# First mixture of experts: the rows of the last expert added by a matrix product, the gather of the others issued before that expert, and the even output projection done by token halves

## The chip, the core and the metric

The kernel runs on one core of a Trainium2 chip, in 32-bit floats. The metric is the device time of one execution in microseconds (us). Engines are named as in the profile: PE multiplies matrices (PEld is its weight load), DVE and ACT are the vector and scalar engines, POOL issues the indirect transfers, SP issues most of the weight loads.

## What is computed

Two networks run on 256 tokens each, one behind the other. The second has two blocks, and in its first block 256 latent and 256 context tokens go through an "even" mixer, whose output projection is added to the token stream, and then through a mixture of 16 experts, of which each token takes two. The change lies in that first block.

```python
def moe(h, router_w, router_b, w1, w3, w2):
    scores = jax.nn.sigmoid((h @ router_w).astype(jnp.float32))
    ...                                        # two experts of the best group of four, and their shares
    y = jnp.zeros_like(h)
    for e in range(N_EXPERTS):
        y = y + comb[:, e:e + 1] * ((jax.nn.silu(h @ w1[e]) * (h @ w3[e])) @ w2[e])
    return y

# second_block, l = 0
        x_lat = x_lat + g1 * o_lat             # o = [attention heads, mLSTM heads] @ w_out
        h_lat = modulate(x_lat, norm_ffn_g[l], sh2, sc2).reshape(B * S, D)
        ...
            x_ctx = x_ctx + cg1 * o_ctx
            h_ctx = modulate(x_ctx, norm_ffn_g[l], csh2, csc2).reshape(B * L, D)
            y = moe(jnp.concatenate([h_lat, h_ctx], axis=0), router_w, router_b, exp_w1[l], exp_w3[l], exp_w2[l])
            y_lat = y[:B * S]
            x_ctx = x_ctx + cg2 * y[B * S:].reshape(B, L, D)
        x_lat = x_lat + g2 * y_lat.reshape(B, S, D)
```

`modulate` is a root-mean-square norm over the 1024 features, times a gain, plus a shift.

## The kernel before

Each engine runs an instruction list written out by hand in program order; semaphores connect them. An engine never passes an instruction that waits. The token stream is `x_t`, features on partitions in eight blocks of 128, 512 tokens along the row: columns 0 to 255 are the context half, 256 to 511 the latent half. PSUM is used as four families of two banks, `proj`, `score`, `turn` and `outp`. `claim(f)` on PE takes the next bank of a family once the bank's earlier use is drained, and `take(f)` on a reader waits until it is filled. Weights of 1 MB come through a ring of six slots that SP fills in order. SP may load a slot again when its last reader is done.

**Even output projection** (`slot_out`, `out_projection`). Each of four ring slots holds 256 output columns, so PE runs two banks of 512 tokens for each, 16 matmuls (32 recorded instructions, since a matmul of 32-bit floats is recorded as two). DVE adds each bank, gated, to `x_t` (`add_gated`, L2770). ACT squares the new `x_t`; PE sums the squares over features with ones (L732, L739); ACT takes the root; DVE takes the reciprocal and multiplies, in two halves of 256 tokens (`normalise`, L2339 and L2583); ACT applies gain and shift (`shift`, L1944). Only then comes the router's product (L1490), then ACT's copy of the logits (L1760), four small matmuls and the sigmoid (L1760 again), and on DVE a chain of some forty small steps that picks two experts for each token, gives it a row in each expert's list (`row_of`, up to 96 rows for an expert) and counts.

**First mixture** (`experts(0)`). POOL scatters the tokens' rows to `xrow_d` in HBM (`expert_in`), and loads them again expert by expert. SP waits until the first such load has landed before it loads expert 1's weights. For each expert PE does `gate` (into `proj`), `hidden` of the up weights (into `score`), `act_turned` (transposes the product) and `output` (into `outp`, rows of 96 tokens packed in four strips of 32 partitions, L1348). Expert e's output stands behind the up product of expert e+1. SP loads gate, up and then the previous expert's output weights (L3281), each when the same place in the ring was last used. The last two loads are expert 15's output weights, issued when its gate product is done. ACT copies each expert's rows (`rows_out`) and stores them to `yrow_d` (`expert_out`).

**After the last expert** POOL waits for all stores, then issues eight indirect gathers (two for each block of 128 tokens, in the order 2, 3, 0, 1, latent first) into `h_tok` and `y_two`. ACT scales one (L2220), DVE adds the other (`mix`, L3037), PE transposes (`mixed_turned`, L1663), DVE adds to `x_t` (`add_mixed`, L3047). The latent half is normed first; then the next block's input projection starts: six steps c = 0 to 5 of one PE product each. At c = 0 the context half's norm follows the product. From c = 1 on, `turn_pairs(c - 1)` follows it: sums of squares for head c - 1 and a rotation product (L664, into `outp`), from which DVE (L3074, L3076, L3077, a reciprocal L2589, L3086) makes the finished head and signals `head_ready`. SP loads these products' weights (`in_odd_w_in`, L3263) once all four blocks are mixed.

If an expert is chosen by more than 96 tokens, a branch (`overflow`) handles the rest. Each engine reads the count and branches (L1311 on PE).

## Time and profile before

| | us |
|---|---|
| median of the 3 runs | 1568.49 |
| lowest, highest | 1566.29, 1568.64 |
| the profiled execution | 1571.42 |
| its span in the trace | 1569.7 |
| PE busy | 1460.4 (93%) |
| DVE, ACT, POOL busy | 560.5, 346.3, 99.5 |

Busy time of an engine says how much it does, not whether anybody waits for it. The chain that ended last names, step by step, what released the next instruction; the timeline gives starts and lengths. Times of day below are microseconds from the span's start. The granted clock stands in the rows as a share of full speed: 1.00 is 2.4 GHz, 0.50 is 1.2 GHz.

The stretches that matter here: the even output projection runs from about 714 to 780, norm and routing to about 816, the 16 experts to about 1112, the gather and mixing to about 1143, and the projection steps c = 0 to 5 to about 1203.

### The profile page before, as it was taken

The page shows a single profiled execution, that of the slowest core. Times are in us where ns is not written, and L with a number is a line of the kernel's source. Part 1 is how long each engine was busy: PE and PEld are TensorE (multiplying, and loading weights), DVE is VectorE, ACT ScalarE, POOL GpSimd, SP SyncE. Part 2 cuts the span into 40 slices and gives each one's busy share as a digit, 9 for nine tenths or more (in the row PEclk, how much of TensorE's full clock was granted, in tenths as well). Part 3 has the DMA queues.
Part 4 walks back from the last instruction along what each step waited for, and adds up shares of the span by engine and source line. Part 5 has one row for each costly group of instructions (what it writes and reads, how often), then busy time and mean ns, then how long its engine had stood idle before and what let it go on. Part 6 is the DMA issues. An engine that isn't in the chain of part 4 may idle for free.

```text
span 1569.7 us, 27108 instructions
## 1 busy us (share of the span) xinstructions
PE 1460.4 (93%) x11433; PEld 1036.6 (66%) x11433; DVE 560.5 (36%) x1380; ACT 346.3 (22%) x804; POOL 99.5 (6%) x152
## 2 busy tenths in 40 slices
PE   7999999999999999999967999999599989899997
PEld 5687677876744767564346999989365666555554
DVE  2615412355155157253150111111266823233233
ACT  2313302133231132262040000100242313000010
POOL 0010100100300000220010000000200001000000
PEclk9999999999999999999979999999799999999999
DMA  8463763735964610655218999999591055999997
GB/s 283 115 215 108 228 195 100 230 120 192 297 205 149 202 54 28 215 182 197 81 64 322 363 399 400 391 398 408 195 364 64 1 187 199 383 382 393 376 384 282
DMA packets 189275, 367.05 MB, mean 234 GB/s; under 512 B 20140, under 2 KB 146952, under 8 KB 173312
## 3 DMA queue, kind: packets, MB, share of 16 engines
q1 hardware_dynamic: 172736, 323.30, 58.3%
q0 software_dynamic: 10544, 32.48, 6.5%
q10 hardware_dynamic: 5904, 9.98, 1.7%
q8 instruction: 66, 1.08, 0.3%
q14 instruction: 25, 0.20, 0.0%
HBM read 345.33 MB, written 20.41 MB: 233 GB/s over the span
## 4 chain that ended last, share of the span: by engine, by line
PE 78%; DMA 10%; DVE 6%; ACT 3%; issue 2%; POOL 1%; SPq 0%; POOLq 0%; ACTq 0%; DVEq 0%
PE ps_proj L664 29%; PE ps_proj L1348 8%; PE ps_outp L664 7%; PE ps_outp L1348 7%; PE ps_score L1348 6%; DMA ring<-in_exp_w 6%; PE ps_outp L1293 4%; PE ps_outp L1449 2%; PE ps_score L848 1%; PE ps_turn L827 1%; PE ps_proj L800 1%; PE ps_proj L912 1%; PE ps_proj L1198 1%; DMA expert_in<-arena,row_of 1%; PE ps_score L908 1%
## 5 line engine op out<-in xcount | busy, mean ns | idle before, releaser
L664 PE MATMUL ps_proj<-h_t,ring 128*128 128x256 f32 (+1 forms) x1184 | 323.8, 431 | 6.5 <-DVE h_t L2437 3.9
L664 PEld LDWEIGHTS ps_proj<-h_t,ring 128*128 128x128 f32 x1184 | 224.8, 192 | 97.6 <-issue 68.4
L1348 PE MATMUL ps_proj<-ring,arena 128*32 128x384 f32 (+2 forms) x1760 | 118.8, 387 | 7.9 <-DMA ring<-in_exp_w 4.9
L1348 PEld LDWEIGHTS ps_proj<-ring,arena 128*32 128x32 f32 (+1 forms) x1760 | 103.9, 115 | 23.6 <-issue 9.9
L1348 PE MATMUL ps_score<-ring,arena 128*32 128x384 f32 (+2 forms) x1760 | 115.1, 381 | 4.1 <-DMA ring<-in_exp_w 4.1
L1348 PE MATMUL ps_outp<-ring,arena 128*32 128x384 f32 (+2 forms) x1504 | 112.7, 417 | 3.5 <-DVE arena L2794 2.1
L1348 PEld LDWEIGHTS ps_score<-ring,arena 128*32 128x32 f32 (+1 forms) x1760 | 98.2, 113 | 20.4 <-issue 8.7
L664 PE MATMUL ps_proj<-ring,h_t 128*128 128x256 f32 x448 | 100.4, 381 | 0.4 <-ACT arena L1969 0.4
L1348 PEld LDWEIGHTS ps_outp<-ring,arena 128*32 128x32 f32 (+1 forms) x1504 | 81.8, 114 | 27.1 <-DVE arena L2794 3.8
L664 PEld LDWEIGHTS ps_proj<-ring,h_t 128*128 128x128 f32 x448 | 84.1, 190 | 15.6 <-issue 4.8
L1760 ACT ACTIVATE arena<-ps_proj 128x512 f32<-128x512 f32 (+1 forms) x68 | 38.5, 569 | 248.9 <-PE ps_proj L664 241.6
L2819 DVE TENSOR_TENSOR arena<-ps_outp,arena 128x512 f32<-128x512 f32 x62 | 40.0, 687 | 94.4 <-PE ps_outp L1449 94.4
L2996 DVE COPY arena<-ps_score 128x384 f32<-128x384 f32 x16 | 8.9, 558 | 152.4 <-PE ps_score L1603 152.4
L2589 DVE RECIPROCAL rstd<-root 128x512 f32<-128x512 f32 x14 | 46.9, 3353 | 43.2 <-ACT root L1760 43.0
L1293 PE MATMUL ps_outp<-arena,ring 128*128 128x512 f32 x128 | 57.8, 609 | 3.0 <-DVE x_t L2770 2.1
L3118 POOL DMA_DIRECT2D modulation_parts<-ada_out x48 | 27.1, 567 | 514.4 <-ACT ada_out L1823 514.4
L664 PE MATMUL ps_outp<-h_t,ring 128*128 128x256 f32 x256 | 56.7, 381 | 2.2 <-DMA ring<-in_w_out 1.4
L664 PEld LDWEIGHTS ps_outp<-h_t,ring 128*128 128x128 f32 x256 | 48.2, 190 | 10.2 <-issue 3.9
L2193 ACT ACTIVATE arena<-ps_outp 128x384 f32<-128x384 f32 x32 | 15.7, 490 | 171.7 <-PE ps_outp L1348 171.7
L1293 PEld LDWEIGHTS ps_outp<-arena,ring 128*128 128x128 f32 x128 | 24.6, 195 | 35.3 <-issue 34.3
L1766 ACT ACTIVATE h_t<-x_t 128x512 f32<-128x512 f32 (+1 forms) x28 | 18.3, 685 | 125.9 <-DVE x_t L2770 60.9
L1811 ACT ACTIVATE both_probs<-ps_score,negmax 128x128 f32<-128x128 f32 (+1 forms) x64 | 30.7, 483 | 65.6 <-DVE negmax L2409 39.4
(403 smaller groups left out, 1848.9 us busy)
## 6 DMA issues: line engine op xcount, KB each, us to landing
ring<-in_exp_w SPq DMA_DIRECT2D x138, 1024.0 KB, 11.4
ring<-in_ada_w SPq DMA_DIRECT2D x48, 1024.0 KB, 5.5
ring<-in_w_in SPq DMA_DIRECT2D x30, 1024.0 KB, 6.5
arena<-in_exp_w SPq DMA_DIRECT2D x24, 1024.0 KB, 15.4
ring<-in_even_w_in SPq DMA_DIRECT2D x12, 1024.0 KB, 6.5
ring<-in_w_out SPq DMA_DIRECT2D x8, 1024.0 KB, 10.1
row_store<-in_exp_w SPq DMA_DIRECT2D x8, 1024.0 KB, 15.6
x_t<-in_exp_w SPq DMA_DIRECT2D x16, 512.0 KB, 15.7
```

Of the source, the lines that this page charges most:

```text
L664: last = pe.matmul(out, w, a, start=(i == 0), stop=(i == len(pairs) - 1))
L800: last = pe.matmul(b[q:q + 32, half * 256:(half + 1) * 256], cond[:, k, :], w[:, k, :], start=(k < 4), stop=(k >= 4))
L1293: last = pe.matmul(b[c][:, :], w[:, k, c * P:(c + 1) * P], nq_t[:, k, :] if k < 4 else ym_t[:, k - 4, :], start=(k == 0), stop=(k == 7))
L1348: last = pe.matmul(b[p0:p0 + pn, c0:c0 + wn], x_of(p0, lo, pn), w(w0, wn), start=first and p0 not in strip[:i], stop=done and p0 not in st ...
L1449: pe.matmul(b[:, :], pick_t[at:at + 64, t * P:(t + 1) * P], y_rows[at:at + 64, 0:512], start=True, stop=True).then_inc(filled[f], 1)
L1760: act.activation(out, src, func, **kw).then_inc(drained["proj"], 1)
L1766: act.activation(h[:, 2 * q:2 * q + 2, :], x_t[:, 2 * q:2 * q + 2, t0:t0 + n], ACT.Square).then_inc(sq_ready, 1)
L1811: ins = act.activation(dst[:, lo:hi], b[:, lo:hi], ACT.Exp, scale=sign, bias=negmax[:, u % 2, q:q + 1], accum_out=total[:, u % 2, q:q + 1])
L2193: act.activation(y_rows[:, q * wide:(q + 1) * wide], bank["outp"][(o0 + q) % 2][:, 0:wide], ACT.Copy).then_inc(drained["outp"], 1)
L2589: step(dve.reciprocal(rstd[:, :], root[:, i % 2, :]))
L2819: dve.tensor_tensor(o, b[:, :], o, ALU.add).then_inc(drained[f], 1)
L3118: pool.dma_start(ada_d[k // 12, s, :, i * 512:(i + 1) * 512], ada_out[s:P:32, k % 2, :]).then_inc(ada_stored[k % 2], 16)
```

## The change

It has four parts.

1. In the even output projection slot 0 is as before. For slots 1 to 3 all context halves come first, then all latent halves, 256 tokens in one bank each. Sums, norm, shift and the transposes of the context half are put between and behind the latent products; behind the end only the latent half is left. The sigmoid's small matmuls go ahead of the remaining transposes.
2. Expert 15's output goes into 96 partitions times two banks of 512 columns (`last_output`: three strips instead of four), is copied to `y_rows` and stays there. DVE builds, ahead of the expert loop, a slot-by-token matrix of the shares of expert 15 (`last_apart`), PE transposes it (`last_pick_turned`), and PE adds `y_rows` times that matrix in PSUM (`last_rows`), together with the other rows, which are turned by a matmul with the identity (`other_rows`). Tokens of expert 15 get share 0 in the gather and a row of another expert.
3. POOL gathers when the 15 other experts are stored. To have these rows early, PE does expert 14's output ahead of expert 15's up product. SP waits for the latent gathers only, and for the mixing before the later weights.
4. The mixing works on halves of 256 tokens. The context half is mixed behind the product of c = 0, and its norm stands behind c = 1 instead of c = 0. ACT takes up that norm at c = 2, once head 0 is finished.

```diff
+            def half_sums(s):
+
+                b = claim("proj")
+                for q in range(4):
...
+            for i in range(1, 4):
+                w = out_weights(i)
+                b = claim("outp")
+                out_part(b, w, HALF[0], 0)
+                out_part(b, w, HALF[0], 1).then_inc(filled["outp"], 1)
+            for i in range(1, 4):
+                w = slot_view((out_slot + i) % RING, KC, 256)
+                b = claim("outp")
+                out_part(b, w, HALF[1], 0)
+                if i == 2:
+                    sum_quarters(S)
+                out_part(b, w, HALF[1], 1).then_inc(filled["outp"], 1)
+                done_with("outp")
+                if i == 1:
+                    half_sums(0)
+            mark["x_even"] = use["outp"]
+            pe.wait_ge(ctx_shifted, KC)
+            tokens_turned(0)
+            half_sums(1)
+            squared[0] += 8
+            sum_quarters(S, S)
+            tokens_turned(1)
...
+                        for q in range(2):
+                            if half == 0:
+                                pe.wait_ge(drained["outp"], o0 + q - 1 + 2 * e)
+                            parts = [(p, 32, p, 0, 512 * q, 512) for p in (0, 32, 64)]
+                            for k in (2 * half, 2 * half + 1):
+                                last = strips(bank["outp"][(o0 + q) % 2], parts, act_of(k),
...
                 gate(e)
                 act_turned(e - 1)
+                output(e - 1)
+                use["turn"] += 2 * EXPERTS
+                last_pick_turned()
                 hidden(e, "score", 2)
-                output(e - 1)
                 act_turned(e)
-                output(e, True)
+                last_output(e)
...
+            def last_rows(s, p):
+
+                f, lo = MIX_BANKS[p], S * (1 - s)
+                b = claim(f)
+                for j in range(2):
+                    c = (2 * p + j) * P
+                    pe.matmul(b[:, j * S:(j + 1) * S], y_rows[0:CAP[0], c:c + P], last_pick_t[0:CAP[0], lo:lo + S],
+                              start=(j == 0), stop=False)
+                mark["mix", s, p] = use[f]
...
+            def other_rows(s, banks):
+
+                for i in range(2):
+                    pe.wait_ge(mixed, 2 * s + i + 1)
+                    for p in range(4):
+                        for j in range(2):
+                            c = (2 * p + j) * P
+                            last = pe.matmul(banks[p][:, j * S + i * P:j * S + (i + 1) * P],
+                                             h_tok[:, TOKEN_BLOCKS[2 * s + i], c:c + P], ident, start=False,
...
             experts(0)
-            for i in range(3):
-                mixed_turned(i)
-            norm(h2[:, :, S:T2], S)(0, 4)
-            mixed_turned(3)
+            banks = [last_rows(0, p) for p in range(4)]
+            other_rows(0, banks)
+            lat_norm = norm(h2[:, :, S:T2], S)
+            banks = []
+            for p in range(4):
+                banks.append(last_rows(1, p))
+                lat_norm(p, p + 1)
...
                 if c == 0:
-                    norm(h2[:, :, 0:S], S)(0, 4)
+                    other_rows(1, banks)
                 if c >= 1:
                     turn_pairs(c - 1)
+                if c == 1:
+                    norm(h2[:, :, 0:S], S)(0, 4)
...
+                    half_square(2, 0, 1)
+                    half_square(2, 0, 0)
+                    for q in range(1, 4):
+                        half_square(2 + q, q, 1)
+                    evac(root[:, 1, 0:S], n=S)
+                    half_square(6, 1, 0)
+                    evac(root[:, 0, 0:S], ACT.Sqrt, S, scale=1.0 / D, bias=EPS)
+                    half_square(7, 2, 0)
+                    for c in range(KC):
+                        xn[0] += 1
+                        act.wait_ge(xn_ready, xn[0])
+                        act.activation(h[:, c, 0:S], h[:, c, 0:S], ACT.Identity, scale=gain[:, 0, 1, 1, c:c + 1],
+                                       bias=mod[:, 0, 3 * KC + c, 1:2]).then_inc(ctx_shifted, 1)
+                    tokens_out(0, 0)
+                    half_square(8, 3, 0)
+                    tokens_out(0, 4)
+                    evac(root[:, 1, S:T2], n=S)
+                    evac(root[:, 0, S:T2], ACT.Sqrt, S, scale=1.0 / D, bias=EPS)
+                    for c in (0, 4):
+                        tokens_out(1, c)
+                    shift(h, 0, 1, S, 1)
+                    warm_up(ACT.Sigmoid)
+                    b = take("score")
+                    act.activation(logit_t[:, 0:n], b[:, 0:n], ACT.Copy).then_inc(drained["score"], 1)
...
-                rows_out(EXPERTS - 1)
+                e = EXPERTS - 1
+                act.wait_ge(y_stored, 32 * e)
+                for q in range(2):
+                    act.wait_ge(filled["outp"], o0 + q + 1 + 2 * e)
+                    act.activation(y_rows[0:cap, q * 512:(q + 1) * 512], bank["outp"][(o0 + q) % 2][0:cap, :], ACT.Copy
+                                   ).then_inc(drained["outp"], 1)
...
+            def stream_weighted(s):
+
+                for t in TOKEN_BLOCKS[2 * s:2 * s + 2]:
+                    act.wait_ge(gathered[t], 32)
+                    act.activation(h_tok[:, t, :], h_tok[:, t, :], ACT.Identity, scale=part[:, 0, t:t + 1]
...
+            stream_weighted(0)
+            stream_squares(0)
             rms_root(S)
             stream_shift(0)
-            stream_squares(1, mark["moe_done", 0])
+            stream_weighted(1)
             for c in range(6):
                 if c == 1:
+                    stream_squares(1)
+                if c == 2:
+                    act.wait_ge(head_ready, 9)
                     rms_root(S)
...
+            for i in range(1, 4):
+                add_half(i, 1)
+            add_half(1, 0)
+            normalise_half(1)
+            add_half(2, 0)
+            add_half(3, 0)
...
+                def last_apart():
...
+                    step(dve.scalar_tensor_tensor(out=row_f, in0=away, scalar=-float((EXPERTS - 1) * CAP[0]), in1=row_f,
+                                                  op0=ALU.mult, op1=ALU.add))
+                    dve.tensor_copy(row_back[:, :, :], row_f).then_inc(back_ready, 1)
+                    step(dve.tensor_tensor(away_part, away, part, ALU.mult))
+                    dve.tensor_tensor(part, part, away_part, ALU.subtract).then_inc(part_ready, 1)
...
+                    for t in range(nb):
+                        ins = dve.tensor_scalar(last_pick[:, t, :], cst("slot")[:, 0:cap], last_place[:, t:t + 1],
+                                                last_share[:, t:t + 1], ALU.is_equal, ALU.mult)
...
                 rows_in(2)
+                last_apart()
...
+                use["turn"] += 2 * EXPERTS
+                b = take("turn")
+                dve.tensor_copy(last_pick_t[0:cap, :], b[0:cap, :]).then_inc(drained["turn"], 1)
...
             experts(0)
             mix(0)
             mix(1)
             add_mixed(0)
+            normalise(h2[:, :, S:T2], S)
             mix(2)
+            mix(3)
             add_mixed(1)
...
             for c in range(6):
+                if c == 1:
+                    for cols in rms(S):
+                        for k in range(KC):
+                            dve.tensor_tensor(h2[:, k, 0:S], x_t[:, k, 0:S], rstd[:, cols], ALU.mult).then_inc(xn_ready, 1)
...
-                pool.wait_ge(y_stored, 32 * EXPERTS)
+                pool.wait_ge(back_ready, 1)
...
-                    gather(yrow_d[0:EXPERTS * CAP[l], :])
+                    pool.wait_ge(y_stored, 32 * (EXPERTS - 1))
+                    gather(yrow_d[0:(EXPERTS - 1) * CAP[l], :])
...
             for entry, n in zip(stream, first_slot):
                 if entry == "early":
+                    sp.wait_ge(filled["outp"], mark["moe_done", 0])
                     for i in range(EARLY):
                         block_load(n, i)
                     continue
...
                 if l == 0:
-                    sp.wait_ge(mixed, T2 // P)
+                    sp.wait_ge(gathered[TOKEN_BLOCKS[1]], 32)
```

The order of instructions shows three places. The first is PE behind the output projection's third slot. `h_t` holds the squares, L674 of the changed program is the plain product (before, L1293), L742 and L749 are the sums (before, L732 and L739). Before:

```order
L1293 MATMUL ps_outp<-arena,ring 128x512 [waits outp_drained,ring_loaded1,proj_drained]
L1293 MATMUL ps_outp<-arena,ring 128x512 x15
L732 MATMUL ps_proj<-h_t,const 32x512 [waits sq_ready]
L732 MATMUL ps_proj<-h_t,const 32x512
L1293 MATMUL ps_outp<-arena,ring 128x512 [waits outp_drained,ring_loaded2]
L1293 MATMUL ps_outp<-arena,ring 128x512 x15
```

Changed, from the last latent product on:

```order
L674 MATMUL ps_outp<-arena,ring 128x256 [waits outp_drained]
L674 MATMUL ps_outp<-arena,ring 128x256 x7
L749 MATMUL ps_proj<-root,const 128x256 [waits proj_drained]
L674 MATMUL ps_outp<-arena,ring 128x256 x8
L674 MATMUL ps_outp<-arena,ring 128x256 [waits outp_drained]
L674 MATMUL ps_outp<-arena,ring 128x256 x15
L1323 MATMUL ps_proj<-const,h_t 128x128 [waits proj_drained,ctx_shifted]
```

The context half's sum now stands inside the products, and its transposes directly behind them.

The second place is PE at expert 15. `ring_loaded5` and `ring_loaded0` are the up weights of expert 15, `ring_loaded1` and `ring_loaded2` the output weights of expert 14; rows that continue a product are left out. Before:

```order
L1603 MATMUL ps_score<-const,arena 128x128 x2
L1348 MATMUL ps_score<-ring,arena 32x384 [waits ring_loaded5]
L1348 MATMUL ps_score<-ring,arena 32x384 x2
...
L1348 MATMUL ps_score<-ring,arena 32x384 [waits ring_loaded0]
...
L1348 MATMUL ps_outp<-ring,arena 32x384 [waits outp_drained,ring_loaded1,score_drained]
L1348 MATMUL ps_outp<-ring,arena 32x384 x2
```

Changed:

```order
L1667 MATMUL ps_score<-const,arena 128x128 x2
L1404 MATMUL ps_outp<-ring,arena 32x384 [waits outp_drained,ring_loaded1,score_drained]
...
L1404 MATMUL ps_outp<-ring,arena 32x384 [waits ring_loaded2]
...
L1691 MATMUL ps_turn<-const,arena 96x128 [waits turn_drained,last_pick_ready]
L1691 MATMUL ps_turn<-const,arena 96x128 x3
L1404 MATMUL ps_score<-ring,arena 32x384 [waits ring_loaded5]
```

The product that needs the weights loaded later now stands ahead of the one whose weights are loaded first.

The third place is ACT and PE at steps c = 1 and 2 of the projection. ACT, changed: `root<-ps_proj 128x512` finishes head 0's root; the two rows behind it are the context norm, `head_ready` is DVE's signal that head 0 is done.

```order
L2060 ACTIVATE arena<-ps_proj 128x512 [waits proj_filled]
L2421 ACTIVATE arena<-ps_proj,vec 128x512
L1867 ACTIVATE root<-ps_proj 128x512 [waits proj_filled,head_ready]
L1867 ACTIVATE root<-ps_proj 128x256 [waits proj_filled,head_ready]
L1867 ACTIVATE root<-ps_proj 128x256 [waits proj_filled]
L2392 ACTIVATE h_t<-h_t,mod,gain 128x256 [waits xn_ready] x8
```

PE, changed, from `turn_pairs(0)` on; `proj_drained` of L749 is the first of these two ACT rows:

```order
L674 MATMUL ps_proj<-arena,const 128x512 [waits proj_drained,head_sq_ready]
L674 MATMUL ps_outp<-arena,const 128x512 [waits outp_drained,proj_drained]
L742 MATMUL ps_proj<-h_t,const 32x256 [waits sq_ready,proj_drained]
...
L749 MATMUL ps_proj<-root,const 128x256 [waits proj_drained]
L674 MATMUL ps_proj<-h_t,ring 128x256 [waits proj_drained,ring_loaded5]
L674 MATMUL ps_proj<-h_t,ring 128x256 x15
```

Before, the ACT rows of the same norm stood ahead of head 0's root, with no wait for `head_ready`:

```order
L1953 ACTIVATE arena<-ps_proj 128x512 [waits proj_filled]
L2253 ACTIVATE arena<-ps_proj,vec 128x512
L1760 ACTIVATE root<-ps_proj 128x256 [waits proj_filled] x2
L2237 ACTIVATE h_t<-h_t,mod,gain 128x256 [waits xn_ready] x8
L1953 ACTIVATE arena<-ps_proj 128x512 [waits proj_filled]
```

The context norm moved behind head 0, and PE's product of c = 2 stands behind that norm's second sum.

## Rows read from the trace of the kernel before

**Rows 1.** The chain that ended last: start, us, engine, result, line, instructions
```profile
831.87 3.69 DMA arena<-expert_in
...
1121.62 6.14 DMA arena<-expert_out,row_of
...
1143.61 7.52 PE ps_proj L664 x32
...
1278.24 7.12 PE ps_outp L664 x32
```

**Rows 2.** Timeline, output projection: start, us, instruction, count, idle before
```profile
751.51 13.97 PE L1293 MATMUL ps_outp<-arena,ring 128*128 128x512 f32 x32 [1.06 <-DVE x_t L2770]
...
780.56 0.88 DVE L2770 SCALAR_TENSOR_TENSOR x_t<-ps_outp,mod,x_t 128x256 f32<-128x256 f32 x2 [2.56 <-PE ps_outp L1293]
```

**Rows 3.** Timeline, end of the second half's shift, and the sigmoid
```profile
793.59 4.04 ACT L1944 ACTIVATE h_t<-h_t,mod,gain 128x256 f32<-128x256 f32 x8 [0.43 <-DVE h_t L2583]
...
801.41 0.22 ACT L1760 ACTIVATE arena<-ps_proj 128x64 f32<-128x64 f32 x1 [0.43 <-PE ps_proj L1503]
```

**Rows 4.** SP's two loads of expert 14's output weights (line L3281, 1089.7 to 1091)
```profile
L3281 SPq DMA_DIRECT2D ring<-in_exp_w x2: 383/384/384, 1089.5 to 1090.1; - x2
...
DMA to landing us min/median/max: 9.7/10.7/11.8
```

**Rows 5.** Timeline of PE: expert 15 up, expert 14 output, expert 15 output
```profile
1094.98 5.45 PE L1348 MATMUL ps_score<-ring,arena 128*32 128x384 f32 x96
...
1100.16 5.46 PE L1348 MATMUL ps_outp<-ring,arena 128*32 128x384 f32 x80
...
1106.75 5.41 PE L1348 MATMUL ps_outp<-ring,arena 128*32 128x384 f32 x80 [0.65 <-DVE arena L2996]
```

**Rows 6.** Timeline, then windows: length, busy by engine, clock, DMA, GB/s
```profile
859.62 7.10 PE L1348 MATMUL ps_proj<-ring,arena 128*32 128x384 f32 x96 [3.80 <-DMA ring<-in_exp_w]
...
859.00:860.00 1.00, 0.38 (x5) 0.34 (x9) 0.00 (x0) 0.00 (x0) 0.00 (x0) 0.82 0.95 393
...
1113.00:1143.00 30.00, 9.80 (x50) 6.47 (x50) 13.51 (x31) 9.06 (x13) 7.93 (x8) 0.60 0.62 209
```

**Rows 7.** Timeline of PE, expert 0: up product, then its output with nothing between
```profile
826.03 5.50 PE L1348 MATMUL ps_score<-ring,arena 128*32 128x384 f32 x96
...
833.45 5.41 PE L1348 MATMUL ps_outp<-ring,arena 128*32 128x384 f32 x80 [0.65 <-DVE arena L2996]
```

**Rows 8.** PE's branch on the count: lengths in ns, starts
```profile
L1311 PEldq COMPARE_BRANCH  x2: 340/398/456, 1113.8 to 1567.2; - x2
```

**Rows 9.** Timeline, gathers, mixing and the latent norm
```profile
1117.78 1.01 POOL L3249 DMA_INDIRECT arena<-expert_out,row_of  x1 [50.38 <-issue]
...
1124.48 1.15 ACT L2220 ACTIVATE arena<-arena 128x1024 f32<-128x1024 f32 x1 [11.78 <-DMA arena<-expert_out,row_of]
...
1125.74 1.28 DVE L3037 SCALAR_TENSOR_TENSOR arena<-arena 128x1024 f32<-128x1024 f32 x1 [19.04 <-ACT arena L2220]
...
1134.24 1.28 ACT L1793 ACT_TABLE_LOAD   x1
...
1135.64 2.17 ACT L1766 ACTIVATE h_t<-x_t 128x512 f32<-128x512 f32 x4
...
1138.98 0.38 ACT L1760 ACTIVATE root<-ps_proj 128x256 f32<-128x256 f32 x1 [1.17 <-PE ps_proj L732]
...
1142.86 4.05 ACT L2237 ACTIVATE h_t<-h_t,mod,gain 128x256 f32<-128x256 f32 x8 [2.28 <-DVE h_t L2583]
```

**Rows 10.** Timeline, norm sums; c = 2 and head 0's rotation
```profile
1151.05 1.07 PE L732 MATMUL ps_proj<-h_t,const 128*32 128x256 f32 x16
...
1161.81 7.07 PE L664 MATMUL ps_proj<-h_t,ring 128*128 128x256 f32 x32
1162.08 0.69 DVE L3074 TENSOR_TENSOR arena<-ps_outp,const 128x512 f32<-128x512 f32 x1 [3.72 <-PE ps_outp L664]
...
1167.65 0.69 DVE L3086 TENSOR_TENSOR arena<-arena,rstd 128x512 f32<-128x512 f32 x1
```

249 lines of the change are left out of this document (162 added, 87 removed).

## Prediction

> **What bounds the kernel now.** I read the chain that ended last first. It says who releases whom in the stretches that the change touches: PE's output projection, then ACT and DVE through norm and routing, then the scattered rows coming back from HBM (a load of 3.69 us that ends at 835.56), PE and the weight loads through the experts, the last gather (6.14 us, landed at 1127.76), and PE again from the projection's first product at 1143.61 [rows 1]. So there are two places where PE waits for others: 45 us between the output projection's end at 780.5 and expert 0's up product at 826.0 [rows 2, 7], and 31 us between expert 15 and that first product. A microsecond saved ahead of the scatter starts SP's loads for expert 1 earlier and moves everything behind by the same. The second view is the timeline of both places, the third SP's loads with their time to landing, since the experts run close to the weight stream and the change turns two products round there.
>
> I keep the times of day of the trace and follow PE to its product of step c = 2, which starts at 1161.81 [rows 10]. From there PE's list is the old one.
>
> **Part 1, the output projection by halves.** Slots 1 to 3 take 13.97 us each and wait 1.06 for DVE's add [rows 2], since both banks are in use: 45.1 in all. Six halves of 32 instructions at 7.12 [rows 1] are 42.7, and with one bank each nothing waits, for a half's add is 0.88 us [rows 2] beside 7.12. The context half's sums (1.07 [rows 10]) and its second sum (0.45 by the same rate) stand between them: 44.2, a gain of 0.9.
>
> Behind the last product there were 17.1 us until the shift's end, 780.5 to 797.6 [rows 2, 3]: squares and sums of 512 columns, then reciprocal, multiplications and shift (4.04) for one half after the other. Now one half is left, but copies of transposed rows stand between its steps on ACT: add 0.9, a copy 0.6, the square 0.5, last sums 0.3, another copy 0.3, then as in [rows 9] 3.9 from the sums' end to the shift's start (1138.98 to 1142.86), and 4.05 of shift: 10.6. Gain 6.5. The small matmuls no longer stand behind eight transposes: before 3.8 us from the shift's end to the sigmoid [rows 3], now 1.4 for the table load, 0.6 copy, 1.0 matmuls: gain 0.7. DVE does one step more (0.2) ahead of the row numbers. Sum: 7.9 us earlier, all of it passed on through the scatter. The bounds are 6 (if the context shift ends after the last product and holds PE) and 9.
>
> **Part 2, expert 14's output ahead of expert 15's up product.** At 1095.0 the up product of expert 15 begins [rows 5]. Now output 14 stands there. Its weights were issued at 1089.5 and 1090.1 and landed 9.7 and 11.8 us later, at 1099.2 and 1101.9 [rows 4]. Before, PE came to them at 1100.2 and did not notice. SP's list is unchanged and the stream is full, so PE now waits 4.2 us. After a wait of 3.80 us the granted clock fell (0.82 in the mean of that microsecond) and the next product took 7.10 us instead of 5.46 [rows 6]: 1.6 more. Output 14 ends at 1106.4, 0.8 later than before, and up 15 still stands behind it: with 0.5 for the four transposes and 5.45 for the product, 1112.4.
>
> The cover of the turned activations is gone too. Between up and output PE had output 14 to do; now it is as at expert 0, 831.53 to 833.45 [rows 7], 1.9 us: 1114.3. The last output is three strips of 512 columns instead of four of 384, 5.41 x 4/3 = 7.2: it ends at 1121.5. Before, 1112.2 [rows 5]. **PE's last expert ends 9.3 us later.** (If the weights were there in time this would be 3.5.) The Trainium skill, page "TensorE: Matmul & The Clock Gate", section "Measured speedup vs the span model", measured 2.38 times for three column tiles; by it the last output would take about 9.1 and the end be 1.9 later. The trace's four strips ran at 5.41 us for 16 passes of 384 columns, which by the full-width rate of [rows 2] (13.97 for 32 of 512) are 5.24 unpacked, so packing costs 3% here, and I keep 7.2.
>
> **Part 3, the gather under expert 15.** Rows of expert 14 are copied at 1107 and stored; by 1106.9 the weight stream has ended, so some 3 us: POOL starts at about 1110.5 instead of 1117.78, and the second block's gather landed 10.0 us after the first issue [rows 1, 9], now at 1120.5. Who needs it? ACT, but ACT has the last expert's copy (0.6) and the count's branch ahead. PE passed its branch 2.1 us after its last product (1112.16 to 1114.25) [rows 5, 8], so 1123.6. Then the table load, 1.4 until the next instruction [rows 9]: 1125.0. The gather has 4.5 us to spare, and this much of what it won is not used. The table load was hidden under a scatter-wait before and is now on the path. The Trainium skill, page "ScalarE: Activation LUTs", section "What ACT_TABLE_LOAD costs", puts a table switch at about 2.66 us with a drain; the time of the first product would be 1.3 later by it. The trace has 1134.24 to 1135.64, and I go by that.
>
> ACT scales two blocks at 1.15, DVE mixes them at 1.28 [rows 9]: ready at 1127.5 and 1128.8. PE does the rows of expert 15 for the latent half meanwhile (16 instructions of 256 columns at 0.22 [rows 1], 3.6 us) and then 32 of 128 columns at 0.11 to 0.13: done at 1131.5. DVE's adds run in step. The context half's rows of expert 15 now stand between the latent sums, four times 0.9 + 0.3: 1136.3. From there 4.5 to the first product, as before (1138.98 to 1143.4 [rows 9]): **1140.8 instead of 1143.61**, a gain of 2.8 out of a gather that took 14.
>
> **Part 4, steps c = 0 and c = 1.** The product of c = 0 takes 7.52 [rows 1]. Behind it come 32 instructions for the context rows (3.9) that were not in PE's stream before, but no norm. Product c = 1 (7.1) ends at 1159.3, before 1160.3. And now the norm: PE's second sum needs ACT's copy, and ACT makes it only when head 0 is finished. Head 0 takes DVE 6.3 us from the rotation's end (1162.08 to 1168.34) [rows 10]; before, this lay beside the product of c = 2. Now rotation ends at 1161.2, head 0 at 1167.5, copy 0.4, sum 0.9 at the low clock: product c = 2 starts at 1168.8, 7.0 later than 1161.81, and after more than 5 us of waiting it pays the 1.6 of [rows 6] again. **8.6 us later.**
>
> DVE's preparation of the matrix (13 small steps, under 3 us) lies in a stretch where it waits for PE, and costs nothing. SP asks for the projection's weights when the latent gathers are in and the last output is done, at 1121.5, almost 20 us ahead of their first product.
>
> **The sum.** 7.9 earlier, 8.6 later: 0.7 us slower. The profiled execution's 1571.42 (span 1569.7) would be 1572.1; the median of the three runs is 2.9 lower than that execution, so 1568.5 + 0.7 = 1569.2 us. Both terms are known to about 2 us. Measurement tells changes of 0.2%, 3.1 us: below 1565.4 is faster, above 1571.6 slower.
>
> **Rivals.** (a) The sum above, 0.57. (b) Output 14 finds its weights: SP or the stream is faster at that point, for instance because nothing is loaded behind them. Against it: landing times of 9.7 to 11.8 us at a stream that never paused. PE would save 5.8; the gather, then landed at about 1122, holds ACT and gives back nearly 2: 1565.2. 0.13. (c) Slower by the clock: PE works in short bursts between 1123 and 1141, and in the old kernel, with 9.8 us of work in the 30 between 1113 and 1143, the granted clock was 0.60 in the mean [rows 6]. For it: the waits at output 14 and behind the sums. Against it: PE now comes from a full product and never rests over 3 us before 1136. If the granted clock is 0.50 there, the 16, 32 and 16 instructions double, 3 + 4 + 3 us less what ACT hides, some 6 to 8: 1576. 0.12. (d) Part 1 pays less: the context half's shift stands on ACT ahead of the last latent square, and if it ends 2 or 3 us behind the last product, it holds transposes, square and sums in a row: 1572. 0.10. (e) Both waits for the clock are cheaper and part 1 gives 9: 1564.5. 0.07. (f) An expert over 96 tokens, so that nothing is gathered early: no overflow instruction is in the trace; 0.01.
>
> Faster 0.20, same 0.57, slower 0.23. The range is 1563.5 to 1575: it takes in (b), (d), (e) and half of (c).
>
> **What would show it.** Right: a PE wait of about 4 us for `in_exp_w` ahead of expert 14's output; 1.9 us between up 15 and its output; the last output near 7.2 us; gathers landed before ACT asks; a PE wait of 6 us on the norm's copy behind c = 1; routing 8 us earlier. Wrong: an expert loop that doesn't start 8 us earlier, no PE wait at output 14, or ACT's copy for the context norm ahead of head 0's end.

## The result

The changed kernel takes 1575.78 us (median of 18 runs, 1570.63 to 1578.86); the kernel before, beside it, 1568.57 (18 runs). The ratio is 1.0043, 95% interval 1.0034 to 1.0052: 6.7 us slower (5.3 to 8.2), where the forecast had 0.7. Where this text gives a gain or a loss of a kernel in us, it is worked out from the ratios. The profiled execution took 1576.11, its span is 1574.5.

The two profiled executions differ by 3 us ahead of the region of the change: slot 0 of the projection ends at 735.42 before and at 732.4 after. So times of day can't be set side by side. I measure part 1 from the end of slot 0, and all behind it from **G**, the start of the transposes of expert 14's activations, directly behind expert 15's gate product: 1094.50 before (0.5 ahead of the first row of [rows 5]), 1081.30 after.

**Part 1**, timeline of the changed kernel (start, us, instruction, count, idle before), the lines that answer to [rows 2, 3]: last products and add, the latent shift, the sigmoid, the row numbers.

```profile
767.77 7.72 PE L674 MATMUL ps_outp<-arena,ring 128*128 128x256 f32 x35
...
775.53 0.88 DVE L2950 SCALAR_TENSOR_TENSOR x_t<-ps_outp,mod,x_t 128x256 f32<-128x256 f32 x2 [4.60 <-PE ps_outp L674]
...
781.94 4.04 ACT L2051 ACTIVATE h_t<-h_t,mod,gain 128x256 f32<-128x256 f32 x8 [0.94 <-DVE h_t L2961]
...
789.14 0.22 ACT L1867 ACTIVATE arena<-ps_proj 128x64 f32<-128x64 f32 x1 [1.15 <-PE ps_proj L1565]
...
802.52 0.17 DVE L3156 CAST row_of<-arena 128x8 uint32<-128x8 f32 x1
```

The last product ends 43.1 us behind slot 0's end (45.1 before), then come 10.5 to the shift's end (17.1), 3.2 to the sigmoid (3.8) and 13.4 to the row numbers (12.7): 70.1 instead of 78.7. The gain of part 1 is there in the trace, 8.6 us.

**Behind G**, the same view, lines that answer to [rows 5, 9, 10].

```profile
1085.67 8.17 PE L1404 MATMUL ps_outp<-ring,arena 128*32 128x384 f32 x80 [3.83 <-issue]
...
1099.37 1.01 POOL L3467 DMA_INDIRECT arena<-expert_out,row_back  x1 [45.30 <-DMA expert_out<-arena]
...
1101.70 7.07 PE L1404 MATMUL ps_outp<-ring,arena 128*32 128x512 f32 x48 [0.65 <-DVE arena L3195]
...
1110.72 1.08 ACT L2364 ACTIVATE arena<-ps_outp 96x512 f32<-96x512 f32 x2 [16.33 <-remote]
...
1113.32 3.78 PE L1750 MATMUL ps_turn<-arena 96*128 96x256 f32 x8 [4.54 <-issue]
...
1162.45 0.38 ACT L1867 ACTIVATE root<-ps_proj 128x256 f32<-128x256 f32 x1 [6.41 <-DVE arena L3304]
...
1162.89 1.22 PE L749 MATMUL ps_proj<-root,const 128*128 128x256 f32 x2 [5.83 <-ACT root L1867]
...
1163.91 8.32 PE L674 MATMUL ps_proj<-h_t,ring 128*128 128x256 f32 x32
```

SP's loads of output 14's weights, with the time to landing (the profile calls PE's wait for them "issue"):

```profile
L3501 SPq DMA_DIRECT2D ring<-in_exp_w x2: 383/383/383, 1076.3 to 1076.9; - x2
DMA to landing us min/median/max: 9.3/10.3/11.3
```

From the chain that ended last, the first product of the projection:

```profile
1134.37 9.49 PE ps_proj L674 x32
```

PE waits 3.8 us ahead of output 14, and goes on at 1085.67, when the first of the two loads has landed (1076.3 + 9.3). That output takes 8.17 us instead of 5.46. The first eight records of the last expert's rows (`last_rows`, L1750) take 3.78, where five profiles below have 1.99. The first product takes 9.49 instead of 7.52 [rows 1]. Ahead of the product of c = 2 PE waits 5.8 us for ACT's copy, and the product takes 8.32 instead of 7.07 [rows 10]. The windows view (length, busy time with count of each engine, granted clock, DMA share, GB/s) shows these four places at a mean clock of 0.57, and full clock in the stretch between the first two:

```profile
1084.00:1092.00 8.00, 6.33 (x55) 4.72 (x59) 0.00 (x0) 0.00 (x0) 0.00 (x0) 0.57 0.93 374
1111.00:1119.00 8.00, 5.68 (x14) 4.58 (x15) 2.48 (x2) 4.36 (x6) 0.00 (x0) 0.57 1.06 374
1132.00:1140.00 8.00, 5.63 (x15) 4.62 (x16) 5.16 (x11) 6.12 (x10) 0.00 (x0) 0.57 0.02 6
1159.00:1167.00 8.00, 4.11 (x11) 3.36 (x12) 5.79 (x5) 0.95 (x3) 0.00 (x0) 0.57 0.02 9
1092.00:1111.00 19.00, 15.40 (x181) 9.02 (x173) 1.80 (x3) 1.26 (x3) 7.67 (x8) 1.00 0.56 187
```

### The profile page after: what moved, and what is told of

It reads as the page before. It is cut to its first block, busy times and chain, and to the rows that moved or that the text cites. A ratio compares the mean times of both kernels' runs of the same rounds, so it can differ in the third digit from the quotient of the medians.

```text
span 1574.5 us, 27439 instructions
## 1 busy us (share of the span) xinstructions
PE 1475.2 (94%) x11599; PEld 1067.6 (68%) x11599; DVE 562.1 (36%) x1379; ACT 347.8 (22%) x810; POOL 99.5 (6%) x152
## 4 chain that ended last, share of the span: by engine, by line
PE 78%; DMA 9%; DVE 5%; ACT 4%; issue 2%; another core or an unknown queue 1%; SPq 1%; POOL 0%; ACTq 0%; POOLq 0%; DVEq 0%
PE ps_proj L674 29%; PE ps_outp L674 10%; PE ps_proj L1404 7%; DMA ring<-in_exp_w 7%; PE ps_outp L1404 6%; PE ps_score L1404 6%; PE ps_outp L1505 2%; PE ps_score L858 1%; PE ps_turn L837 1%; PE ps_proj L810 1%; PE ps_proj L922 1%; SPq L3501 1%; PE ps_proj L1208 1%; PE ps_score L918 1%
## 5 line engine op out<-in xcount | busy, mean ns | idle before, releaser
L674 PE MATMUL ps_proj<-h_t,ring 128*128 128x256 f32 (+1 forms) x1184 | 325.7, 433 | 7.4 <-DVE h_t L2605 4.0
L674 PEld LDWEIGHTS ps_proj<-h_t,ring 128*128 128x128 f32 x1184 | 227.3, 194 | 97.3 <-issue 70.7
L1404 PE MATMUL ps_outp<-ring,arena 128*32 128x384 f32 (+3 forms) x1472 | 117.0, 431 | 7.8 <-issue 3.8
L674 PE MATMUL ps_proj<-ring,h_t 128*128 128x256 f32 x448 | 100.3, 381 | 0.4 <-ACT arena L2076 0.4
L674 PEld LDWEIGHTS ps_proj<-ring,h_t 128*128 128x128 f32 x448 | 84.1, 190 | 15.7 <-issue 4.8
L1867 ACT ACTIVATE arena<-ps_proj 128x512 f32<-128x512 f32 (+3 forms) x67 | 38.0, 570 | 248.1 <-PE ps_proj L674 240.1
L674 PE MATMUL ps_outp<-arena,ring 128*128 128x256 f32 x320 | 70.2, 380 | 0.4 <-DVE arena L3308 0.4
L674 PEld LDWEIGHTS ps_outp<-arena,ring 128*128 128x128 f32 x320 | 60.6, 190 | 9.9 <-issue 0.9
L674 PE MATMUL ps_outp<-h_t,ring 128*128 128x256 f32 x256 | 56.7, 381 | 2.4 <-DMA ring<-in_w_out 1.6
L674 PEld LDWEIGHTS ps_outp<-h_t,ring 128*128 128x128 f32 x256 | 48.2, 190 | 10.4 <-issue 4.1
L3190 DVE TENSOR_TENSOR arena<-arena,ps_score 128x384 f32<-128x384 f32 x16 | 8.9, 554 | 94.4 <-PE ps_score L1404 94.4
## 6 DMA issues: line engine op xcount, KB each, us to landing
ring<-in_exp_w SPq DMA_DIRECT2D x138, 1024.0 KB, 11.4
```

What stands on the lines that cost most here:

```text
L674: last = pe.matmul(out, w, a, start=(i == 0), stop=(i == len(pairs) - 1))
L1404: last = pe.matmul(b[p0:p0 + pn, c0:c0 + wn], x_of(p0, lo, pn), w(w0, wn), start=first and p0 not in strip[:i], stop=done and p0 not in st ...
L1867: act.activation(out, src, func, **kw).then_inc(drained["proj"], 1)
```

## The experiments

All ratios are to the kernel before, measured beside each. This table, read from the timelines, gives PE's progress in us behind G; c = 2 is the product of that step. Columns: end of the last output, start of the first product, start and length of c = 2, then the measured ratio with its interval. The kernel changed_again is the changed kernel measured and profiled a second time; its section stands at the end.

| kernel | last output | first product | c = 2 | ratio |
|---|---|---|---|---|
| before | 17.7 | 49.1 | 67.3, 7.07 | 1 |
| halves_only | 17.7 | 49.5 | 67.7, 7.07 | 0.9958 (0.9943 to 0.9973) |
| changed | 27.5 | 53.1 | 82.6, 8.32 | 1.0043 (1.0034 to 1.0052) |
| changed_again | 27.5 | 49.9 | 79.4, 8.32 | 1.0032 (1.0021 to 1.0044) |
| tail_only | 26.1 | 48.3 | 77.1, 9.64 | 1.0078 (1.0065 to 1.0091) |
| swap_alone | 24.0 | 55.4 | 75.0, 7.07 | 1.0038 (1.0024 to 1.0052) |
| up_first | 19.8 | 44.0 | 73.5, 8.32 | 0.9992 (0.9983 to 1.0000) |
| norm_first | 26.1 | 48.1 | 71.2, 7.07 | 1.0016 (1.0008 to 1.0025) |
| rows_in_gap | 26.4 | 51.4 | 69.5, 7.07 | 0.9958 (0.9943 to 0.9973) |
| waits_filled | 27.0 | 53.5 | 80.5, 7.07 | 1.0031 (1.0020 to 1.0042) |
| filled_late | 26.2 | 50.2 | 77.2, 7.07 | 1.0007 (0.9998 to 1.0015) |
| all_three | 19.8 | 43.5 | 61.7, 7.07 | 0.9909 (0.9893 to 0.9926) |
| all_three_fill | 19.8 | 44.3 | 62.5, 7.07 | 0.9920 (0.9908 to 0.9932) |

The changed kernel stands there twice, 1.0043 and 1.0032. Against the second measurement every gain over it that is given below is 1.7 us smaller.

**The change cut in two.** halves_only is the kernel before with the even projection by halves, tail_only the kernel before with all the rest.

> The kernel before with part 1 alone (even output projection by token halves, with its norm, copies and router product); gather, mixing and norms as before. Theory A (part 1 pays in full and the loss lies behind expert 15): expert 15's gate ends about 10 us earlier than before when both profiles are set to the same start of the projection, so 8 to 10 us faster than before, near 1559.5. Rival B (the experts are bound by the weight stream, which takes most of it back): less than 4 us faster, 1565 or more. The forecast had 7.9.

> The kernel before with parts 2 to 4 alone (expert 14's output ahead of expert 15's up product, rows of expert 15 by the matrix, early gather, mixing by halves, norm behind head 0); output projection as before. Theory A: the whole loss stands here, 15 to 17 us slower than before, near 1585. Rival B: 9 us slower at most, near 1577, as the forecast's own sum has it (8.6), and the rest is an interplay with part 1.

They take 1562.26 and 1582.57, the kernel before 1569.88: 6.6 us faster (4.2 to 8.9) and 12.2 slower (10.2 to 14.3). In sum that is 5.6 slower, the change as measured within its intervals. Both are smaller than theory A had (8 to 10, and 15 to 17) and larger than rival B's bounds (4 and 9). So part 1 pays and keeps most of its pay: from the row numbers to G the experts take 281.4 us, before 280.4, and in the other kernels with part 1 from 278.8 to 282.8. The whole loss stands behind expert 15's gate, and it is 12, not 8.6.

**Part 2 by itself.**

> The kernel before with one exchange on PE alone: expert 14's output ahead of expert 15's up product, four strips as before, gather as before. It measures part 2 of the forecast by itself. The forecast's terms: 4.2 of waiting for weights, 1.6 for the low clock, 1.9 for the uncovered turn of the activations: 7.7 us slower, near 1577.5. Rival: the rival (b) of the forecast (the weights are there in time), 2 us slower, near 1572.

```diff
+                output(e - 1)
                 hidden(e, "score", 2)
-                output(e - 1)
                 act_turned(e)
                 output(e, True)
```

It takes 1574.56, 6.0 us slower (3.8 to 8.2). Its timeline (G at 1090.50):

```profile
1094.81 7.09 PE L1348 MATMUL ps_outp<-ring,arena 128*32 128x384 f32 x80 [3.76 <-issue]
...
1109.05 5.41 PE L1348 MATMUL ps_outp<-ring,arena 128*32 128x384 f32 x80 [0.65 <-DVE arena L2996]
```

There is a wait of 3.8, a product 1.6 longer, and then 0.9 more ahead of the last output, for the turned activations that output 14 had covered: the last output ends 6.3 later behind G than before. The mechanism is the forecast's, and its rival (b) falls. The expectation's 7.7 counted the 1.9 us between the up product and the last output in full, though 1.1 of them stood there before too [rows 5].

**The two orders turned back in the changed kernel.**

> The changed kernel with one order turned back: on PE expert 15's up product stands ahead of expert 14's output again (the four transposes of the share matrix go ahead of both). The gathers start about 6 us later. Theory A (the wait for output 14's weights and the uncovered turn of activations cost more than the early gather gives): no PE wait at output 14 and no low clock there, the last output ends 7 to 8 us earlier, ACT's first scaling may wait a little for the gather; 5 to 8 us faster than the changed kernel, near 1569. Rival B (the late gather takes it back): within 2 us of the changed kernel.

```diff
-                output(e - 1)
                 use["turn"] += 2 * EXPERTS
                 last_pick_turned()
                 hidden(e, "score", 2)
+                output(e - 1)
                 act_turned(e)
```

It takes 1569.31, 8 us faster than the changed kernel. The last output ends 7.7 us earlier, and the first product comes 6 us earlier than in changed_again. Its gather and ACT's scaling of the second block:

```profile
1097.74 1.01 POOL L3467 DMA_INDIRECT arena<-expert_out,row_back  x1 [42.48 <-DMA expert_out<-arena]
...
1107.36 1.15 ACT L2401 ACTIVATE arena<-arena 128x1024 f32<-128x1024 f32 x1 [1.62 <-DMA arena<-expert_out,row_back]
```

The expectation had the gathers about 6 us later, and that did not come. Behind G they start at 15.4, and in the kernels with the turned order and the same early gather at 15.0 to 18.1 (before: 23.3). So the exchange on PE did not bring the rows forward. The forecast's own numbers say as much, for they have output 14 end at 1106.4 instead of 1105.6. What makes the gather early is that it no longer waits for expert 15's rows. In the old order ACT waits 1.6 us for the second block, but DVE has it mixed at 1109.8 and PE turns it from 1113.0 on, so in this profile the rows are in time.

> The changed kernel with the context half's norm ahead of head 0 on PE, ACT and DVE (still behind the product of c = 1). Theory A (PE stands at the norm's second sum because ACT's copy waits for head 0, and pays for the low clock behind it): the wait of 5.8 us goes, the product of c = 2 runs at full clock, 6 to 8 us faster than the changed kernel, near 1568.5. Rival B (head 0 is then late for the later steps and the product of c = 3 waits as long): less than 3 us faster.

```diff
+                if c == 1:
+                    norm(h2[:, :, 0:S], S)(0, 4)
                 if c >= 1:
                     turn_pairs(c - 1)
-                if c == 1:
-                    norm(h2[:, :, 0:S], S)(0, 4)
```

(ACT's and DVE's lists to match.) It takes 1572.08, 4.2 us faster than the changed kernel, which is between the two theories; beside the second measurement it is 2.5, within rival B. Against changed_again PE's product of c = 2 starts 8 us earlier, but the product of c = 3 only 7, and it is 1.7 longer:

```profile
1163.99 0.69 DVE L3303 TENSOR_TENSOR arena<-arena,rstd 128x512 f32<-128x512 f32 x1
1164.78 0.60 ACT L2060 ACTIVATE arena<-ps_proj 128x512 f32<-128x512 f32 x1 [4.26 <-DVE arena L3303]
...
1166.09 8.72 PE L674 MATMUL ps_proj<-h_t,ring 128*128 128x256 f32 x32 [2.47 <-ACT arena L2417]
```

ACT's copy of the c = 2 product waits for DVE's finished head 0, which now stands behind the norm, and the product of c = 3 waits for that copy's bank and runs at the low clock.

> The changed kernel with the context half mixed in the gap ahead of the projection's first product (its 32 row matmuls stand behind the latent norm's second sum, ACT scales and DVE mixes these blocks before the latent root), and the context norm at c = 0 as in the kernel before. Theory A (the gap of 3.4 us at the first product has room for the 3.9 us of rows, and with the norm back at c = 0 nothing waits for head 0): 3.5 from the rows, 6 to 7 from the norm's wait and the clock behind it, 9 to 10 us faster than the changed kernel, near 1566. Rival B (head 0 is the limit whatever the order, as with the norm ahead of head 0 alone, which gained 4): 5 to 6 us faster, near 1570.

```diff
                 lat_norm(p, p + 1)
+            other_rows(1, banks)
             ready = mixer_input()
...
                 if c == 0:
-                    other_rows(1, banks)
+                    norm(h2[:, :, 0:S], S)(0, 4)
```

(ACT's and DVE's lists to match.) It takes 1563.03, 13 us faster than the changed kernel, more than theory A had. The context rows now fill the 3.4 us in which PE waited for the latent shift, so the first product also runs at full clock, 7.50 us. The expectation had given that no price.

**The low clock by itself.** Into waits of PE I put matmuls whose result nobody reads.

> The changed kernel with matmuls that nobody reads put into four waits of PE: 4 of 512 columns (0.87 us each) ahead of expert 14's output, 1 behind the last output, 3 ahead of the projection's first product, 6 ahead of the context norm's second sum. The waits stay as long, only the low clock behind them can go. Theory A (the low clock behind short waits costs 5 to 6 us in sum: about 1.3 at output 14, 1.5 at the last rows, 2 at the first product, 1.3 at c = 2): 4 to 6 us faster than the changed kernel, near 1571, and no granted clock of 0.5 in 1080 to 1175. Rival B (the low clock falls on work that something else hides): within 1.5 us of it, or slower where a filling matmul overruns its wait.

Its two early places, beside the two late ones that the next diff shows:

```diff
+                fill("turn", 4)
                 output(e - 1)
...
                 last_output(e)
+                fill("score", 1)
```

> The changed kernel with matmuls that nobody reads in two waits of PE alone: 3 ahead of the projection's first product, 6 ahead of the context norm's second sum. Unlike in waits_filled nothing is added ahead of the mixing, so PE's stop inside the mixing rows must stand where it stood. Theory A (the low clock behind these two waits costs time, 1.3 to 2.0 and 1.3 to 2.5): products of 7.5 and 7.1 us at full clock, 3 us faster than the changed kernel. Theory B: within 1 us.

```diff
+            def fill(f, n):
+
+                for i in range(n):
+                    pe.matmul(bank[f][0][:, :], ident, x_t[:, 0, :], start=True, stop=True)
...
+            fill("score", 3)
             ready = mixer_input()
...
-                    norm(h2[:, :, 0:S], S)(0, 4)
+                    norm_sums(h2[:, :, 0:S], S)(0, 4)
+                    fill("score", 6)
+                    sum_quarters(S)
```

filled_late, with the two late places alone, takes 1570.35 beside changed_again's 1574.48, 4 us faster (about 2 to 6 by the ratios' intervals). The waits are as long as before, the first product takes 7.50 instead of 9.47 and c = 2 7.07 instead of 8.32, 3.2 in sum. So the low clock behind these two waits is a cost, and no other work hides it. waits_filled, with all four places, gained only 1.9 where theory A had 4 to 6, though its output 14 ran in 5.41. Part of the reason is that its last output ran at the low clock, which no other profile has:

```profile
1099.53 8.76 PE L1404 MATMUL ps_outp<-ring,arena 128*32 128x512 f32 x48 [0.65 <-DVE arena L3205]
```

The larger part is something else that the filling moved:

**A stop at a fixed place in PE's code.** Timeline of tail_only, filled_late and waits_filled; L1709 and L1767 are the matmuls of `other_rows` in these kernels, L1757 those of `last_rows` in waits_filled.

```profile
1122.36 0.94 PE L1709 MATMUL ps_turn<-const,arena 128*128 128x128 f32 x7
...
1125.04 0.27 PE L1709 MATMUL ps_turn<-const,arena 128*128 128x128 f32 x1 [1.74 <-issue]
```

```profile
1116.62 0.61 PE L1767 MATMUL ps_turn<-const,arena 128*128 128x128 f32 x4
1119.07 0.73 PE L1767 MATMUL ps_turn<-const,arena 128*128 128x128 f32 x4 [1.84 <-issue]
```

```profile
1112.42 0.59 PE L1757 MATMUL ps_outp<-arena 96*128 96x256 f32 x2
...
1117.20 2.44 PE L1757 MATMUL ps_outp<-arena 96*128 96x256 f32 x6 [4.19 <-issue]
```

PE stops 1.7 to 4.2 us in the middle of a run of like matmuls; up_first and norm_first stop as well, 2.1 and 1.5 us, at filled_late's place. In waits_filled five matmuls (10 records) stand ahead of it that filled_late has not, and the stop comes 10 records earlier: 6 of `last_rows` and 4 of `other_rows`. (tail_only, with another projection ahead, stops 3 records later than filled_late.) It hangs on the place in the instruction list, not on data. all_three_fill, below, tests that on the best kernel.

> The kernel rows_in_gap with expert 15's up product ahead of expert 14's output as well, thus the changed kernel with its order turned back in three places. Theory A (the terms add up): another 7 us, near 1559, which is 3 us faster than the output projection's halves alone (1562.3). Rival B (the later gather becomes the limit, PE waits for DVE's mixing at the latent and at the context rows): 1562 or more, no better than the halves alone.

> The kernel all_three with one matmul of 512 columns that nobody reads (0.87 us) behind the last output. In all_three PE idles 2.2 us there, the clock falls to one half, and 16 records of the last expert's rows take 6.9 instead of 3.9 us. Theory A (the clock alone): 2 to 3 us faster than all_three, near 1552. Theory B (PE then comes earlier to the place in its code where it stopped for 1.5 to 2.1 us in three kernels, and where a packet of the instruction queue precedes its going on; in all_three that packet ended at 1110.6, two us before PE came): a stop appears inside the mixing rows and all but 1 us of it is lost again.

all_three takes 1554.59, 14 us less than the kernel before and 8 less than the projection's halves alone. Against the changed kernel the order at expert 15 (up_first) is worth 8 us, the two others (rows_in_gap) 13, and all of them 21, so they add up. Its timeline, last expert's rows at the low clock, then the two products at full clock:

```profile
1105.48 3.78 PE L1750 MATMUL ps_turn<-arena 96*128 96x256 f32 x8 [2.19 <-issue]
...
1109.05 3.52 PE L1750 MATMUL ps_outp<-arena 96*128 96x256 f32 x8
...
1127.04 7.50 PE L674 MATMUL ps_proj<-h_t,ring 128*128 128x256 f32 x32
...
1136.62 7.07 PE L674 MATMUL ps_proj<-h_t,ring 128*128 128x256 f32 x32
```

all_three_fill, 1556.14 (ratio 0.9920), is not faster. The last expert's rows ran at full clock, 1.99 and 1.89, and then:

```profile
1109.49 0.39 PE L1768 MATMUL ps_turn<-const,arena 128*128 128x128 f32 x2
1112.25 1.38 PE L1768 MATMUL ps_turn<-const,arena 128*128 128x128 f32 x6 [2.38 <-issue]
```

One matmul more ahead (2 records), and the stop stands 2 records earlier than in filled_late. In the DMA view of 1109 to 1112 one packet of an instruction queue lies in it (packets, MB, share of 16 engines), none in the 4 us on either side:

```profile
q8 instruction: 1, 0.02, 1.9%
```

I take the packet for PE's code: q8 brought 1.11 MB in this execution, q14, the only other instruction queue, 0.20, and PE has 23202 of the 27442 instructions; no view names the engine. Windows of 0.05 us give the packet's start in every profile. In the six with a stop PE goes on 2.3 to 2.7 us after it, wherever the stop stands. In the four others PE reaches the place about 2.3 to 3.4 us after it, and does not stop. So what the clock gave back PE spent waiting for its code, and behind the stop at the low clock again: the next eight records took 1.91 us instead of 1.06 (theory B). The Trainium skill, page "Runtime: NRT & Kernel Launch", section "Instruction fetch mechanics", says that code is loaded in blocks of 16 KiB in order, mostly unseen, and that a taken branch out of the loaded window makes the engine wait for a load. The traces agree so far: packets of 0.02 MB, and a stop behind PE's branch over the overflow code. No run took the branch away, so that it is the branch that makes the load late is not shown.

**The changed kernel again.** In its first profile ACT's copy came at 1110.72, while the first bank's last matmul, the 36th of the output's 48 records, ends at about 1107.1, and PE stood still for it (the idle 4.54 ahead of L1750 in the first section).

> The changed kernel once more. In its first profile the signals of the last expert's two output banks came 3.6 and 2.0 us behind the recorded ends of their matmuls, and ACT and PE stood still for that. Theory A (this belongs to some executions only; two kernels with the same last output and the same gathers beside it did not show it): ACT copies the first bank at about 5.5 us after the last output's start, and the profiled span is near 1572.5. Theory B (it belongs to the kernel): both signals late again. The time, 1575.8, should repeat within 2 us in either case.

It takes 1574.48. ACT follows at once, at 1112.83 for an output from 1107.36:

```profile
1091.19 8.30 PE L1404 MATMUL ps_outp<-ring,arena 128*32 128x384 f32 x80 [3.76 <-issue]
...
1107.36 7.07 PE L1404 MATMUL ps_outp<-ring,arena 128*32 128x512 f32 x48 [0.65 <-DVE arena L3195]
...
1112.83 0.59 ACT L2364 ACTIVATE arena<-ps_outp 96x512 f32<-96x512 f32 x1 [12.78 <-PE ps_outp L1404]
...
1116.60 2.84 PE L1750 MATMUL ps_turn<-arena 96*128 96x256 f32 x8 [2.17 <-issue]
...
1136.79 9.47 PE L674 MATMUL ps_proj<-h_t,ring 128*128 128x256 f32 x32 [3.44 <-ACT h_t L2392]
```

So the late signal belongs to some executions. It was there in rows_in_gap too, and its cause stays open. The span did not come to theory A's 1572.5: it is 1576.0, though this profile is 3.2 us ahead of the first at the end of c = 2. The difference lies ahead of G, where slot 0's second bank took 8.76 us instead of 7.13 and the way from the row numbers to G 282.8 instead of 278.8.

The two profiles differ at the very end as well. PE's branch behind the second mixture, first profile and second:

```profile
L1365 PEldq COMPARE_BRANCH  x1: 3717/3717/3717, 1570.5 to 1570.5; - x1
```

```profile
L1365 PEldq COMPARE_BRANCH  x1: 444/444/444, 1573.5 to 1573.5; - x1
```

Where this branch is long (3.3 to 3.7 us: changed, tail_only, up_first, norm_first, rows_in_gap, all_three) the span ends 4.7 to 5.0 us behind the chain's last DVE step, in the seven other profiles 3.5 to 3.6. So part of what one profile has over another, about 1.4 us, belongs to the last branch and to none of the orders above. What makes it long in one execution and short in another is open.

## Where the prediction was wrong

I go by its own steps, with changed_again's profile where the first one has the late signal.

- **What bounds the kernel, and 1:1 passing.** Right as far as the noise lets one see. The 8.6 us at the row numbers are 7.8 at G in halves_only's profile, and 6.6 (4.2 to 8.9) in its measured time.
- **Part 1, 7.9.** Right within the interval. The products gave 2.0 instead of 0.9, the end 6.6 (6.5), the small matmuls 0.6 (0.7), and the steps up to the row numbers cost 0.7 instead of 0.2.
- **Part 2, PE's last expert 9.3 later.** Right: it was 9.8. The wait for output 14's weights was 3.8 to 3.9 (4.2), the last output 7.07 (7.2). The term for the low clock was short in some executions: output 14 took 6.7 to 8.3 where about 7.1 was forecast. The price of the strips from the trace's rows held: 16 unpacked passes of 512 columns are 6.99 us by [rows 2], and three strips at once took 7.07, 2.97 times the speed of one after the other. The 2.38 that the Trainium skill's page "TensorE: Matmul & The Clock Gate" (section "Measured speedup vs the span model") has for three column tiles was not seen here.
- **Part 3, from the last output's end to the first product, 19.3. This is the step that failed: it took 22.4**, and 22.3 and 22.0 in tail_only and norm_first; up_first and filled_late, which have the low clock behind the stop as well, took 24.2 and 24.0. PE came back after 2.2 us as forecast (2.1). Then, first, the latent rows ended 11.4 us behind the output and not 10: by the stop in PE's code, or, in changed_again, by the low clock at the last expert's rows (5.3 us for 16 records where 3.6 was forecast), with no stop behind it. The forecast had no term for either. It had no term for code, since the trace of before has PE idle there for 14.9 us, and it had none for the clock, since it took the rest ahead of these rows for too short. Second, the four interleaved steps for sums took 6.3 instead of 4.8: four matmul records of 256 columns take 1.06 to 1.13 and the four records of sums between them 0.56, where I had divided a run of 16 sums (1.07) by four. The gather and ACT's table load (1.28) were in time, as forecast, and nothing of them was on the path.
- **The first product, 7.5.** It took 9.47 at the low clock, behind a wait of 3.4 us that the forecast knew (it is in the 4.5) and to which it gave no price. It had the price of [rows 6] at two waits and left it out at this one. The trace of before even has the same wait of 3.44 us for a shift, ahead of 1292.22, with a granted clock of 0.50 behind it. filled_late shows that it is real time: 2.0 us.
- **Part 4, c = 2.** Right: the wait of 5.8 for ACT's copy behind head 0 (6), and c = 2 1.25 longer (1.6). The change at c = 0 and 1 gave 3.6 for the rows (3.9).
- **The sum.** Behind G the forecast has 83.0 us to the end of c = 2; changed_again has 87.7, before 74.4. The 4.7 are 0.5 of part 2, 3.1 of part 3, 2.0 for the first product, less 0.9 over part 4. With part 1 at 6.6 instead of 7.9 that is 6.0 more than the 0.7 of the forecast, 6.7 in all, and 6.7 was measured. That it meets so closely is partly luck: it adds one execution's profile to the ratio of another kernel, the second measurement has 5.0 (3.3 to 6.9), and the first profile has 3.2 more for the late signal and 1.5 more at the last branch.
- **Rivals.** (c) is what came, in smaller pieces: not one long stretch at half clock but up to four short ones, each behind a wait of 2 to 6 us. "PE now comes from a full product and never rests over 3 us before 1136" was the wrong argument: the rest of 2.2 us behind the last output was followed by the low clock in two of six profiles (all_three, changed_again), the one of 3.4 ahead of the first product in all five that have it. (b) falls by swap_alone. (d) falls by the trace, where the context half's shift ends with the last product (775.52 and 775.49) and part 1 gives its 8.6. (e) falls with the measured time: part 1 did not give 9, and the low clock at output 14 and at c = 2 cost 4.0 us in the first profile where 3.2 were forecast.

## What to carry to other kernels

Give every wait of PE of the lengths seen here (2.2 us in some profiles, 3.4 and more in all) a second price, the low clock behind it, on whatever stands next. Look for real work to put into the wait: here 3.9 us of rows moved into a 3.4 us gap were worth 13 us together with the norm's old place. Before two products are turned round to have data earlier, work out when the data come in either order: here output 14 ended no earlier in the new one, and its weights came later than PE. The matrix for the last expert's rows was good, and with the gather that needs no rows of expert 15 it was worth 8 us beyond the projection's halves, once the orders that it did not need were taken back. New straight-line code behind a branch can meet a stop for its own loading, which no row of the old kernel shows where the engine was idle there.

## What the runs showed of the hardware

- PE stopped 1.5 to 4.2 us inside a run of matmuls behind a branch (six profiles), at a place that moved by exactly as many matmul records as were put ahead of it (0, 2, 10), and went on 2.3 to 2.7 us after the start of a packet of an instruction queue. In the four profiles where the low clock or a late signal made it come later (all_three, changed_again, changed, rows_in_gap) there was no stop.
- PE's branch behind the last mixture took 0.34 to 0.46 us in some executions and 3.3 to 3.7 in others, with the same program (0.44 and 3.72); the span then ended 1.2 to 1.5 us later.
- Behind expert 15's gate a rest of PE of 3.4 to 5.8 us was followed in every profile by the lower granted clock (0.50, 1.2 GHz), one of 2.2 us in two of six. The price varies between executions: output 14, behind the same wait of 3.8, took 6.7 to 8.3 us, the first product 8.8 to 9.5.
- In three of the ten profiles whose gathers run beside the last output (changed, rows_in_gap, waits_filled) the signal of at least one bank came 1.3 to 3.7 us behind the recorded end of its matmuls; in the seven others ACT began its copy 5.5 us after the output's start. What holds them is open.
